# Regrouping the small TensorE blocks of a dilated-attention mixer: scores two phases at a time, value products in one group, in-place transposes

## The reference, cut to what matters

```python
DIL_CONFIGS = ((128, 1), (512, 4), (2048, 16))     # (window, dilation) of the groups
...
    qkv = (h @ w_qkv).reshape(B, T, N_GROUPS_A, 3, HEADS_A, HEAD_DIM)
    for g, (window, dilation) in enumerate(DIL_CONFIGS):
        o, l = dilated_group_attention(qkv[:, :, g, 0], qkv[:, :, g, 1], qkv[:, :, g, 2],
                                       window, dilation, rel_table)
...
    alpha = jax.nn.softmax(jnp.stack(lses, axis=0), axis=0)
    o = jnp.sum(alpha[..., None].astype(h.dtype) * jnp.stack(outs, axis=0), axis=0)
    return o.reshape(B, T, D_MODEL) @ w_o
```

## Time and profile before

| what | value |
|---|---|
| median of 3 runs (range) | 1682.68 us (1681.63 to 1682.94) |
| profiled execution: device time | 1681.54 us |
| profiled execution: span, first to last instruction | 1679.8 us |
| mean granted TensorE clock | 0.994 of full |
| TensorE matmul busy | 98% of the span |
| VectorE, ScalarE, GpSimd busy | 55%, 36%, 4% |
| DMA | 159.66 MB, 33.4% of 16 engines |
| attention steps 1 to 7, from scores to scores | 64.48 to 64.80 us each |
| attention step 8 | 52.47 us |

### The profile page before, as it was taken

How to read it: one execution, slowest core, us unless ns; L and a number is a source line. 1 busy time by engine, 2 the same in 40 slices (tenths; PEclk the granted TensorE clock), 3 DMA queues, 4 the chain that set the end, 5 groups by cost and what they waited for, 6 DMA issues and landing times.

```text
span 1679.8 us, 22173 instructions
## 1 busy us (share of the span) xinstructions
PE 1640.0 (98%) x8285; PEld 1329.4 (79%) x8285; DVE 927.7 (55%) x1625; ACT 612.7 (36%) x1053; POOL 70.4 (4%) x66
## 2 busy tenths in 40 slices
PE   7999999999999999999999999999999999999997
PEld 5878778778777768888888877888867888888886
DVE  6354454554544574444445576777776454545554
ACT  5233243243342342222223444656643222222343
POOL 2000000000000020000000120000020000000111
PEclk8999999999999999999999999999999999999998
DMA  5543343333332233333333334233123333333331
GB/s 150 134 114 99 100 112 100 100 101 92 87 88 68 74 85 90 99 100 87 100 96 92 104 98 112 66 85 97 54 75 94 95 98 102 88 100 92 96 110 66
DMA packets 308312, 159.66 MB, mean 95 GB/s; under 512 B 31156, under 2 KB 303085, under 8 KB 308254
## 3 DMA queue, kind: packets, MB, share of 16 engines
q1 hardware_dynamic: 308254, 158.88, 33.4%
HBM read 156.64 MB, written 10.60 MB: 100 GB/s over the span
## 4 chain that ended last, share of the span: by engine, by line
PE 93%; DVE 4%; ACT 2%; DMA 1%; issue 0%; SPq 0%; POOL 0%; ACTq 0%
PE unit_out L1301 27%; PE unit_out L1303 26%; PE unit_out L1302 26%; PE turned L1377 3%; PE attn L1430 2%; DVE act_lo L957 1%; PE attn L1629 1%; PE logits L1412 1%; PE logits L1301 1%; PE misc L1377 1%; DMA w_raw<-in_a_w_qkv_dram 1%; PE logits L1405 1%; DVE heads L1127 1%; PE logits L1303 1%; PE logits L1302 1%; DVE w_lo L942 1%
## 5 line engine op out<-in xcount | busy, mean ns | idle before, releaser
L1301 PE MATMUL unit_out<-act_hi,w_hi 128*128 128x512 f32 x2024 | 807.2, 399 | 12.1 <-DVE act_lo L957 9.6
L1303 PE MATMUL unit_out<-act_hi,w_lo 128*128 128x512 f32 x2024 | 790.4, 391 | 0.0
L1302 PE MATMUL unit_out<-act_lo,w_hi 128*128 128x512 f32 x2024 | 789.6, 390 | 0.0
L1301 PEld LDWEIGHTS unit_out<-act_hi,w_hi 128*128 128x128 f32 x2024 | 381.1, 188 | 104.4 <-DVE act_lo L957 12.2
L1303 PEld LDWEIGHTS unit_out<-act_hi,w_lo 128*128 128x128 f32 x2024 | 380.5, 188 | 80.9
L1302 PEld LDWEIGHTS unit_out<-act_lo,w_hi 128*128 128x128 f32 x2024 | 381.0, 188 | 77.7 <-issue 2.4
L731 ACT ACTIVATE w_hi<-w_raw 128x1024 fp32r<-128x1024 f32 (+3 forms) x259 | 273.8, 1057 | 440.3 <-PE unit_out L1303 394.1
L942 DVE TENSOR_TENSOR w_lo<-w_raw,w_hi 128x1024 fp32r<-128x1024 f32 (+3 forms) x259 | 323.9, 1251 | 91.2 <-ACT w_hi L731 91.2
L716 POOL TENSOR_TENSOR sumsq<-sumsq,square 128x512 f32<-128x512 f32 x49 | 68.3, 1394 | 1597.8 <-ACT square L749 1596.1
L840 ACT ACTIVATE act_hi<-hidden 128x512 fp32r<-128x512 f32 x64 | 40.5, 633 | 243.2 <-DVE hidden L1146 243.2
L1143 DVE TENSOR_TENSOR scaled<-unit_out,rstd 128x512 f32<-128x512 f32 x64 | 44.1, 690 | 67.8 <-PE unit_out L1303 67.7
(11 more groups left out here) (190 smaller groups left out, 1107.1 us busy)
## 6 DMA issues: line engine op xcount, KB each, us to landing
w_raw<-in_w_ff_dram SPq DMA_DIRECT2D x128, 512.0 KB, 4.0
w_raw<-in_a_w_qkv_dram SPq DMA_DIRECT2D x72, 512.0 KB, 3.8
w_raw<-in_b_w_qkv_dram SPq DMA_DIRECT2D x24, 512.0 KB, 5.2
w_raw<-in_w_ple_gate_dram SPq DMA_DIRECT2D x16, 512.0 KB, 4.0
bias_tiles_b<-bias_vectors SPq DMA_DIRECT2D x16, 256.0 KB, 4.1
bias<-bias_tiles_b SPq DMA_DIRECT2D x8, 512.0 KB, 3.9
w_raw<-in_a_w_o_dram SPq DMA_DIRECT2D x8, 448.0 KB, 3.7
w_raw<-in_b_w_o_dram SPq DMA_DIRECT2D x8, 384.0 KB, 3.4
```

Source lines behind the costliest of these rows:

```text
L1301: te.matmul(bank, w_k[0], hi, start=start, stop=False)
L1302: te.matmul(bank, w_k[0], lo, start=False, stop=False)
L1303: return te.matmul(bank, w_k[1], hi, start=False, stop=stop)
```

## The change

Nothing is computed differently; the same instructions on TensorE stand in another order, some with another PSUM bank.

- **Scores.** Phases 0 and 1 are issued together before the unit of slot 0, phases 2 and 3 together before the unit of slot 2. Even phases write `logits`, odd ones `turned` (`a_bank`).
- **Folds.** Both folds write to the `logits` banks instead of `misc`; the far fold no longer waits for `v_ready`.
- **Transposes.** Phases 2 and 3 are transposed together before the unit of slot 6, phases 0 and 1 before that of slot 8, into `a_bank(ph)`, and the two copies go back into `probs[ph]` itself; `probs_t` is unused here. Phase 2 also waits for `near_share_ready`, phases 0 and 1 for the copies that free their bank.
- **Values.** All four phases' products are one group after the unit of slot 8. `pv_done` is signalled once in a step. `scale_a` keeps its slots.

The diff, blank and unchanged lines left out:

```diff
@@ -60,7 +60,9 @@
...
 A_MERGE = A_ITEMS
-A_VALUES = {5: 2, 6: 3, 7: 0, 8: 1}
+A_SCALES = {4: 2, 5: 3, 6: 0, 7: 1}
+A_TURNS = {6: (2, 3), 8: (0, 1)}
+A_TURN_ORDER = [ph for at_slot in sorted(A_TURNS) for ph in A_TURNS[at_slot]]
@@ -306,6 +308,9 @@
...
+        far_in = logits[:, 0:4 * NT]
+        near_in = logits[:, T:T + 2 * NT]
@@ -326,6 +331,10 @@
...
             return qk_hi[:, o:o + T], qk_lo_a[:, 2 * par + kind, :]
+        def a_bank(ph):
+            return (logits, turned)[ph % 2]
@@ -769,9 +778,11 @@
...
                     next_hi(u)
-                if has_attn and i in A_VALUES:
-                    wait(sc, turned_ready, (s - 1).times(A_ITEMS) + (i - 4))
-                    sc.activation(probs_t[:, 0:T], turned[:, 0:T], ACT.Copy).then_inc(pt_a_ready, 1)
+                if has_attn and i in A_TURNS:
+                    for ph in A_TURNS[i]:
+                        wait(sc, turned_ready, (s - 1).times(A_ITEMS) + (A_TURN_ORDER.index(ph) + 1))
+                        sc.activation(probs[ph][:, 0:T], a_bank(ph)[:, 0:T], ACT.Copy
+                                      ).then_inc(pt_a_ready, 1)
@@ -791,7 +802,7 @@
...
-                    wait(sc, pv_done, s.times(A_ITEMS))
+                    wait(sc, pv_done, s)
@@ -997,7 +1008,7 @@
...
-                ph = A_VALUES[at_slot]
+                ph = A_SCALES[at_slot]
@@ -1012,13 +1023,15 @@
...
                     for cols, low_col, _ in a_segments(i):
-                        to, of, by = probs[i][:, cols], logits[:, cols], a_bias(1 - par, i, cols)
+                        to, of, by = probs[i][:, cols], a_bank(i)[:, cols], a_bias(1 - par, i, cols)
...
                     last.then_inc(logits_done, 1)
-                if has_attn and i in A_VALUES:
-                    wait(ve, turned_ready, (s - 1).times(A_ITEMS) + (i - 4))
-                    ve.tensor_copy(probs_t[:, T:2 * T], turned[:, T:2 * T]).then_inc(pt_b_ready, 1)
+                if has_attn and i in A_TURNS:
+                    for ph in A_TURNS[i]:
+                        wait(ve, turned_ready, (s - 1).times(A_ITEMS) + (A_TURN_ORDER.index(ph) + 1))
+                        ve.tensor_copy(probs[ph][:, T:2 * T], a_bank(ph)[:, T:2 * T]
+                                       ).then_inc(pt_b_ready, 1)
@@ -1031,7 +1044,7 @@
...
                     wait(ve, far_ps, s)
-                    ve.tensor_copy(far_stat[:, :, 0, :], misc[:, 0:4 * NT].rearrange(
+                    ve.tensor_copy(far_stat[:, :, 0, :], far_in[:, :].rearrange(
@@ -1063,10 +1076,10 @@
...
                     wait(ve, near_ps, s)
-                    ve.tensor_copy(near_share[:, :], misc[:, 4 * NT:6 * NT]).then_inc(near_share_ready, 1)
+                    ve.tensor_copy(near_share[:, :], near_in[:, :]).then_inc(near_share_ready, 1)
                     wait(ve, near_share_ready, s)
-                if has_attn and i + 1 in A_VALUES:
-                    scale_a(s, i + 1)
+                if has_attn and i in A_SCALES:
+                    scale_a(s, i)
@@ -1241,7 +1254,7 @@
...
-                    wait(ve, pv_done, t)
+                    wait(ve, pv_done, t - (ITEMS_A - A_PAIRS))
@@ -1402,14 +1415,14 @@
...
                                 rows = slice(j * E, (j + 1) * E)
-                                last = te.matmul(logits[:, j * T + first:j * T + end], q[a][rows, mine],
+                                last = te.matmul(a_bank(ph)[:, j * T + first:j * T + end], q[a][rows, mine],
...
                                 rows = slice(j * E, (j + 1) * E)
-                                last = te.matmul(logits[:, j * T + first:j * T + first + P],
+                                last = te.matmul(a_bank(ph)[:, j * T + first:j * T + first + P],
@@ -1423,10 +1436,10 @@
...
                         to = by_residue(out_rows)[:, :, tile, :]
-                        by = probs_t[:, col:col + P].rearrange("p (r l) -> p r l", r=NT)
+                        by = probs[ph][:, col:col + P].rearrange("p (r l) -> p r l", r=NT)
...
                         g, keys = c + 1, tile
-                        to, by = out_rows[:, tile * P:(tile + 1) * P], probs_t[:, col:col + P]
+                        to, by = out_rows[:, tile * P:(tile + 1) * P], probs[ph][:, col:col + P]
@@ -1434,36 +1447,43 @@
...
                 u = s.times(A_UNITS) + i
-                t = (s - 1).times(A_ITEMS) + i
-                if has_attn and i in A_SCORES:
-                    if i == 0:
-                        wait(te, qk_ready, s.times(2))
-                        if s.reg is None and s.const == 1:
-                            te.wait_ge(ple_ready, 2)
-                    if i == 2:
-                        wait(te, evac_done, s.times(A_UNITS))
-                    wait(te, logits_done, t)
-                    scores_a(par, i).then_inc(scores_ready, 1)
+                items = (s - 1).times(A_ITEMS)
+                if has_attn and i == 0:
+                    wait(te, qk_ready, s.times(2))
+                    if s.reg is None and s.const == 1:
+                        te.wait_ge(ple_ready, 2)
+                    for ph in (0, 1):
+                        scores_a(par, ph).then_inc(scores_ready, 1)
+                if has_attn and i == 2:
+                    wait(te, evac_done, s.times(A_UNITS))
+                    for ph in (2, 3):
+                        wait(te, logits_done, items + (ph - 1))
+                        scores_a(par, ph).then_inc(scores_ready, 1)
...
                         te.wait_ge(fold_ready, NT - 1)
-                    wait(te, v_ready, s.times(GROUPS) if not has_proj else (s + 1).times(GROUPS))
...
                         last = te.matmul(
-                            misc[b * SUB:(b + 1) * SUB, 0:4 * NT].rearrange("p (a r) -> p a r", r=NT),
+                            far_in[b * SUB:(b + 1) * SUB, :].rearrange("p (a r) -> p a r", r=NT),
...
                     last.then_inc(far_ps, 1)
-                if has_attn and i in A_VALUES:
-                    ph = A_VALUES[i]
-                    wait(te, probs_ready, (s - 1).times(A_ITEMS) + (i - 4))
-                    turn(turned, [(col, probs[ph][:, col:col + P]) for _, _, _, col in a_tiles(ph)]
-                         ).then_inc(turned_ready, 1)
+                if has_attn and i in A_TURNS:
+                    for ph in A_TURNS[i]:
+                        n = A_TURN_ORDER.index(ph)
+                        if n == 0:
+                            wait(te, near_share_ready, s)
+                        if n > 1:
+                            wait(te, pt_a_ready, items + (n - 1))
+                            wait(te, pt_b_ready, items + (n - 1))
+                        wait(te, probs_ready, items + (n + 1))
+                        turn(a_bank(ph), [(col, probs[ph][:, col:col + P]) for _, _, _, col in a_tiles(ph)]
+                             ).then_inc(turned_ready, 1)
@@ -1500,15 +1520,17 @@
...
                         last = te.matmul(
-                            misc[r * SUB:(r + 1) * SUB, 4 * NT:6 * NT].rearrange("p (j b) -> p j b", b=NT),
+                            near_in[r * SUB:(r + 1) * SUB, :].rearrange("p (j b) -> p j b", b=NT),
...
                     last.then_inc(near_ps, 1)
-                if has_attn and i in A_VALUES:
-                    wait(te, pt_a_ready, (s - 1).times(A_ITEMS) + (i - 4))
-                    wait(te, pt_b_ready, (s - 1).times(A_ITEMS) + (i - 4))
-                    values_a(par, A_VALUES[i]).then_inc(pv_done, 1)
+                if has_attn and i == A_UNITS - 1:
+                    wait(te, pt_a_ready, items + A_ITEMS)
+                    wait(te, pt_b_ready, items + A_ITEMS)
+                    for ph in A_TURN_ORDER:
+                        last = values_a(par, ph)
+                    last.then_inc(pv_done, 1)
...
```

## The result

The changed kernel takes 1660.71 us, the median of 4 runs (1659.54 to 1663.47), against 1682.16 us of the kernel before (1681.12 to 1682.94, 4 runs beside it). The medians lie 21.4 us apart; the recorded ratio is 0.9881, with a 95% interval of 0.987 to 0.9892: faster by 1.2%, well clear of no change. The forecast was 1666.8 and a range of 1663.8 to 1674.5.

What follows compares the result with a forecast made beforehand. TensorE's own stream was taken as the bound: 2.11 us a step times seven (14.8) plus 1.05 in step 8, 15.8 off the profiled 1681.54, gives 1665.7; the median 1.14 above, 1666.8. Range 1663.8 to 1674.5.

Steps and rivals of the forecast that it cites:

- The far fold: Inner steps: without its wait the fold follows the V transposes by 0.53 instead of 1.36 us, saving 0.83 a step.
- The joined scores: Inner steps, slots 0 and 2: joining phases 0 and 1 saves 0.33 us a step, phases 2 and 3 0.35.
- Transposes and values: Inner steps, later slots: fewer ways into and out of these blocks on TensorE save 0.60 us a step net.
- the other way: Lower bound: an extra 0.3 us a step if units run as fast behind a block as behind a unit, 1664.3.
- Step 8: Last, shorter attention step: joins and old waits save time, a new 1.0 us wait at phase 1's transposes; net 1.05 saved.
- the estimate of 1668.6: Per step 19 changes of array shape become 9; at 0.1 us each, 1.0 a step saved beside the fold's 0.83.
- The weights of slot 7: SP's queue: the transfer lands 6.4 us after issue, ScalarE then waits 0.8 us, at no cost to TensorE.
- the rival on the slower side: Slot 7's weights land 13.6 us after issue and stall each of six steps by 3.2 us: 1686 and more; chance 0.03.
- Seams that cost as much as exits: Rival: a seam between joined blocks of one kind costs the 0.20 us of an exit; 1671 to 1675.4, chance 0.10.
- The wait that comes back: Rival: TensorE waits for scaled probabilities at slot 6 or 8's paired transposes, eating the gain; 1681 to 1684, chance 0.06.

Runs made afterwards that it cites:

- folds_moved: The kernel before with only both folds moved to the logits banks and the wait for the V copy removed; attention stage 498.54 us against 504.63.
- turns_split: The changed kernel with the transposes of phases 2 and 3 apart, in slots 6 and 7; attention stage 484.43 us, 0.26 less than the change.
- flip: The changed kernel with slot 1's V transposes put between the scores of phases 2 and 3 in slot 2; attention stage 487.09 us, 2.4 more than the change.
- values_split: The changed kernel with its value group cut in two, phases 2 and 3 after the unit of slot 7; attention stage 486.04 us against 484.69.
- scores_joined: The kernel before with only the scores in two banks and issued in pairs of phases; attention stage 497.03 us against 504.63.

## Why the prediction was right in direction and too high

**The far fold: right.** 0.83 a step was forecast, 5.8 in seven; folds_moved measured 6.09 us, 0.3 of it from the fold's own way out (0.18 instead of 0.22). Nothing else became late.

**The joined scores: mechanism right, size too small.** Forecast were 0.68 a step and 1.3 in step 8 with its wait, 6.1 us; measured were 7.60. The joined scores of phases 0 and 1 lead on in 1.59 (forecast 1.70). Those of 2 and 3 lead on in 1.99, near the forecast 2.0, but by luck: a seam of 0.105 instead of 0.06 made up for half of the first gap that was left out.

**Transposes and values: mechanism right, size too small.** The value group lasts as forecast, by the two errors that cancel. The transposes do not: sixteen take 1.66 instead of 1.78 and fourteen 1.45 instead of 1.56, for the 0.85 that I took for eight was a block behind value products. Between units it is 0.79.

**The step that failed** is the one that prices an edge by the way in and the way out alone, and with it the bound "the other way". I read the distance from the last start of one kind to the first start of the next. But a block behind another shape is also slower inside, at its first gap: by 0.10 in scores, 0.05 in value products, 0.06 in transposes. I had seen this for the units (5.39 or 5.33 against 5.24) and even had the row for the scores of phase 1, where I noted that the first of five gaps is longer, and left it out of the sum. Joining two blocks, or putting one behind its own shape, saves that gap too. Per inner step the trace gives 0.12 + 0.04 more than forecast at the scores, 0.23 at the transposes, 0.08 at the folds' ways out (the 0.04 that I took off for the near fold was not lost: it leads on in 0.18 before and after), 0.03 at the values and 0.04 at the units. That is the 0.54 between 62.49 forecast and 61.95, and 3.7 us in seven steps. Step 8 gained 1.45 instead of 1.05. Together the stage gained 19.94 where 15.85 was forecast, 4.1 us more. The bound of 0.3 a step was too tight for it and stood on the wrong thing: it let units run faster behind a block, and they do not; the unit behind the scores of phase 2 before and the one behind the joined scores after both take 5.35 from first start to last.

Of the prediction's small sums, nine units are 9 x 24 x 0.2278 = 49.2 us, not 49.0, and the estimate of 1668.6, with 1.05 for step 8, adds up to 1668.8. Nothing rests on either.

**The other 2 us** are scatter between executions, which the profiled ones place in the first 80 us. I set the median 1.14 above the profiled run, as it was before; after, it came 1.1 below it. That offset is no property of the kernel: beside 1661.8, both 1663.5 and 1659.5 stand in the same list. With the later sets (1681.16 of 14 and 1681.11 of 7 runs before, 1661.47 and 1661.52 after) the gain is 19.6 to 19.7 us, close to the 19.94 of the stage. Even without this offset 1681.16 - 15.85 = 1665.3 is 3.8 too high, and that part is the failed step.

**Step 8: the wait right, the gain too small.** TensorE waits 0.91 us before the transposes of phase 1; 1.0 was forecast. The 0.4 that the step gained beyond the forecast is that 0.1 and, for the rest, mostly first gaps, as in the inner steps. The timeline of VectorE and of TensorE there, after, answers to the earlier trace rows:

```profile
553.70 1.23 DVE L953 TENSOR_TENSOR w_lo<-w_raw,w_hi 128x1024 fp32r<-128x1024 f32 x1 [0.47 <-ACT w_hi L740]
554.84 1.14 DVE L1013 TENSOR_SCALAR probs<-probs,w_raw 128x256 f32<-128x256 f32 x4
```

```profile
554.39 0.82 PE L1390 MATMUL logits<-ident,probs 128*128 128x128 f32 x6
...
556.12 1.06 PE L1390 MATMUL turned<-ident,probs 128*128 128x128 f32 x8 [0.91 <-DVE probs L1013]
```

VectorE is no longer held by a copy and begins the weights when ScalarE is done with them, as worked out.

**The weights of slot 7: right.** ScalarE now waits for them, and TensorE does not notice. After, on ScalarE:

```profile
181.15 1.06 ACT L740 ACTIVATE w_hi<-w_raw 128x1024 fp32r<-128x1024 f32 x1 [5.66 <-DMA w_raw<-in_a_w_qkv_dram]
```

The last matmul of unit 5 started at 179.33, and before the change ScalarE followed such a start by 0.4; here it began 1.4 later than that, since the transfer took 6.9 us to land. I had counted 0.8, from a landing after 6.4. There is no line of TensorE's waits for it. The rival on the slower side needed more than 13 us.

**The rivals.** Seams that cost as much as exits: disproved by every joined block (0.12 and 0.105 in the scores, 0.10 in the values, against exits of 0.20). The wait that comes back: only in step 8. The estimate of 1668.6, from the rule that only a change of tiling mode drains TensorE (the Trainium skill, TensorEngine Tiling (Array Packing), Key Properties), counted the right thing and priced it too low. The runs agree with the rule in what costs time (that TensorE drains is not itself to be seen in a trace): turns_split has one more block of the units' own shape and pays 0.04 a step, flip has two more changes of shape and pays 0.34. But 0.1 a change was too little. It was 0.34 / 2 = 0.17 in flip, 0.28 / 2 = 0.14 in values_split, and (7.6 - 0.5) / 8 / 4 = 0.22 in scores_joined, where a change also took the slow start of a unit with it. The whole change agrees: ten changes of shape fewer in an inner step saved 64.60 - 61.95 - 0.83 = 1.82 us, 0.18 each.

**What stays open.** I did not run the joined transposes and values on the kernel before alone. What is left for them, 19.94 - 6.09 - 7.60 = 6.25 us, is a difference and supposes that the three parts add up. The joined scores were never run in one bank. Behind the stage, flip took 1095.65 us, 0.8 less than before and after (1096.58 and 1096.48); TensorE waits there for VectorE's `act_lo` seven times, 7.5 us in all, instead of eight times, 8.2, and why is open. Why a first gap is longer behind another shape, no run shows.

## What to carry to other kernels

Where TensorE is full, count how often its array changes shape, not how many small blocks there are: each change costs some 0.14 to 0.22 us here, at the way in, at the way out, and in the first gap of what follows. Cutting a block of the main stream's shape in two cost 0.04. To price a regrouping, measure the whole block between the same neighbours that it will have, from its first start to the next kind's first start, and not the edges alone. And when executions scatter by more than the effect, cut the stretch that the edit touches out of the profile: here it repeated to 0.01 us over three profiles while the whole time moved by 4.

## What the runs showed of the hardware that I had not expected

- Score instructions start in pairs, 0.006 us apart and 0.105 from pair to pair, so the mean of 0.06 is the length of no single gap. The same sixteen last 1.16 us behind another shape and 1.06 behind their like; eight transposes lead on in 0.85 behind value products and in 0.79 behind a unit.
- Alternating the PSUM bank of successive score blocks, by itself, changed the stage by 0.2 us of 504.6, nearly all of it in the first step.
- The first 80 us of the program vary by 4.5 us between executions (the stage began between 76.98 and 81.46), along with the mean clock granted to TensorE from 10 to 40 us, 0.94 to 0.77. In that stretch TensorE still stands for inputs and for VectorE, and its busy time is 24 to 25 of 30 us.
